# Recurrent mixer: merge levels 1 to 6 as 64x64 diagonal blocks, and half of the convolution's channels for 22 of 31 taps on POOL

## The chip, the cores and the metric

The kernel runs on one core of one Trainium2 chip. The metric is the device time of one execution in microseconds, median of three runs. The engines are TensorE (PE, its weight loads PEld), VectorE (DVE), ScalarE (ACT), GpSimd (POOL) and SyncE (SP, which issues loads).

## The reference, cut to what matters

Two blocks of two layers each work on 256 tokens of 1024 numbers. The change touches one mixer of the second block only, `mixer_ab` of layer 0: a recurrence (RWKV-7) over 8 heads of 64, and beside it a causal depthwise convolution of 31 taps over 512 channels.

```python
def step(state, inp):                       # rwkv7_scan, one token
    r_t, w_t, k_t, v_t, kk_t, a_t = inp
    s_kk = jnp.einsum('bhvk,bhk->bhv', state, kk_t)
    state = (state * w_t[:, :, None, :]
             - s_kk[..., None] * (kk_t * a_t)[:, :, None, :]
             + v_t[..., None] * k_t[:, :, None, :])
    y_t = jnp.einsum('bhvk,bhk->bhv', state, r_t)
    return state, y_t
...
glu = c_val * jax.nn.sigmoid(c_gate)
conv = lax.conv_general_dilated(
    glu, conv_w[:, None, :], window_strides=(1,), padding=[(CONV_WIDTH - 1, 0)],
    dimension_numbers=('NWC', 'WIO', 'NWC'), feature_group_count=D_CONV) + conv_b
y_b = jax.nn.silu(layer_norm(conv, conv_ln_g, conv_ln_b, CONV_LN_EPS))
return jnp.concatenate([y_a, y_b], axis=-1) @ w_out
```

Everything is float32.

## The kernel before, in words

The kernel works in one pass over all layers; nearly all of its time is dense products of weights that stream in (three products each, high and low parts, L2093 to L2095). The recurrent mixer has one stretch of another kind, and it is the one that the change touches.

**The recurrence as block algebra.** The 256 tokens are two blocks of 128. For each block and head the recurrence becomes the inverse of a unit lower triangular 128x128 matrix N. 16 of them (2 blocks, 8 heads) stand in four groups of four: `N_t[g]`, g from 0 to 3, each 128 partitions x 4 x 128. `D_t[g]` and `DT_t[g]` hold the inverse of the diagonal blocks so far and its transpose, `Z_t[g]` a masked product. Level 0 inverts blocks of 2 tokens; level m, from 1 to 6, merges blocks of 2^m into blocks of 2^(m+1). Level 6 joins two halves of 64 to 128, so that levels 1 to 5 never leave the two diagonal 64x64 blocks.

**A step i.** 24 steps, i from 0 to 23, run in an order written out by hand: `merge_group(i)` is 2*(i//12) + i%2 and `merge_level(i)` is i%12//2 + 1, so two groups alternate through their levels, then the other two. Step i consists of: `z_products(i)`, four 128x128 products N by D into a bank (PE); `masked(...)`, which takes the bank through the level's mask into `Z_t` (DVE, L1786); `merge_products(i)`, four products for D and four for DT (PE, `four_products`, L2619; only DT at level 6); `copied(...)`, which takes each into `D_t` and `DT_t` (ACT, L1018). `z_products(i + 2)` waits for D of step i.

**PE's order.** For p from 0 to 10: `merge_products` of 2p and 2p+1, `z_products` of 2p+2 and 2p+3, then other work of the mixer: for p below 6 two `fill`s (Gram matrices, L2609 and L2614, which DVE takes in `take_gram`, L1822 and L1827), after that `first_block_out` (L2644, L2657, L2670, L2650). Then steps 22 and 23 merge, the second block is solved, and the convolution is turned (`convT`, L2719) after a wait for `conv_done`.

**DVE's order.** Per step: `masked`, then some taps of the convolution, then on odd steps two `take_gram`. `tap(j)` is four instructions, one for each group of 128 channels (`ct`), each a `scalar_tensor_tensor` of 128x256 from `gluT` (in `y`) into `conv_o` (in the arena), L1799 (L1796 for j = 0); `taps_at(i)` says how many taps a step has, 31 in all from step 2 to step 21. At step 21 stand `first_state`, the end of the convolution (`conv_done`) and the bonus sum (L1875, `bonus_done`).

**POOL's order.** POOL makes `r_t` (L572, L579, `rk_made`), then waits for `bonus_done` and makes the output's other terms (four products, L572 and L585, `post_made`), then a power for the heads and one for each half of the convolution's norm (`rstd`, L469), for which DVE waits at L1913. The helper `product` waits for its own semaphore after each instruction.

In the masks (`constants()`, c_masks) level m has 128 columns of its own.

Of the kernel before, what the change touches and what calls it, by code (L numbers as in the profile page):

```python
# [83 lines left out]
def program(nc, a, out):  # L84
# [143 lines left out]
    conv_o = part(7168, 4, T)  # L228
    rho = part(8192, TB, RW)
# [35 lines left out]
    merge_m = [pair_m] + [gflat[:, (2 + m) * P:(3 + m) * P] for m in range(6)]  # L265
# [17 lines left out]
    def merge_level(i):  # L283
        return i % 12 // 2 + 1

# [173 lines left out]
    def _(pool):  # L459
# [119 lines left out]
        pool.tensor_tensor(r_t, r_t, both(r_k), ALU.mult).then_inc(SEM["rk_made"], 1)  # L579
        pool.wait_ge(SEM["bonus_done"], c.next("bonus_done"))  # L580
# [40 lines left out]
    def _(act):  # L621
# [394 lines left out]
        def copied(dst, i, at, got, to):  # L1016
            act.wait_ge(SEM[got], c.next(got))
            act.activation(dst[merge_group(i)], bank[at + i % 2][:, :].rearrange("p (a t) -> p a t", a=4), ACT.Copy)\  # L1018
               .then_inc(SEM[to], 1)
# [18 lines left out]
        for i in range(24):  # L1038
            if merge_level(i) < 6:
                copied(D_t, i, 4, "d_mm", "d_ready")  # L1040
            copied(DT_t, i, 6, "dt_mm", "dt_ready")
# [149 lines left out]
    def _(dve):  # L1191
# [600 lines left out]
        def tap(j):  # L1792
            for ct in range(4):
                dve.wait_ge(SEM["dve"], c.so_far("dve") - 3)
# [54 lines left out]
        def taps_at(i):  # L1849
            if i < 2 or i > 21:  # L1850
                return 0
            return 2 if i > 3 and (i % 2 or i in (18, 20)) else 1

        j = 0
        for i in range(24):
            masked(Z_t[merge_group(i)], z_bank[i % 2], merge_m[merge_level(i)], "z_mm", "zp_ready")
# [10 lines left out]
            for _ in range(taps_at(i)):  # L1867
                tap(j)
                j += 1
            if i == 21:  # L1870
# [217 lines left out]
    def _(pe):  # L2088
# [528 lines left out]
        def four_products(bk, left, right, to):  # L2617
            for i in range(4):
                ins = pe.matmul(bank[bk][:, i * P:(i + 1) * P], left[:, i, :], right[:, i, :], start=True, stop=True)  # L2619
            ins.then_inc(SEM[to], 1)  # L2620

        def z_products(i):
            g = merge_group(i)
            if merge_level(i) > 1:
                pe.wait_ge(SEM["d_ready"], c.next("d_ready"))
            four_products(z_bank[i % 2], N_t[g], D_t[g], "z_mm")
# [6 lines left out]
        def merge_products(i):  # L2633
# [4 lines left out]
            if merge_level(i) < 6:  # L2638
                four_products(4 + i % 2, DT_t[g], Z_t[g], "d_mm")
            four_products(6 + i % 2, Z_t[g], DT_t[g], "dt_mm")  # L2640
# [315 lines left out]
```

## Time and profile before

| | us |
|---|---|
| median of 3 runs (lowest, highest) | 2383.51 (2381.48, 2385.42) |
| the profiled execution | 2382.13 |
| its span | 2380.3 |
| busy in the span: PE, DVE, ACT, POOL | 2335.3, 1788.5, 1197.8, 120.6 |

The span runs from the first to the last instruction of the core; the execution's own time has 1.8 us more around it. A line of the timeline names start, length, engine, line of the kernel, operation, destination and sources, and how many instructions are joined in it; in brackets stands the idle time before it and who ended it. Times are microseconds from the span's start. An instruction's length on DVE and ACT runs beside the start of the next one, so that joined lines are shorter than the sum of their parts.

### The profile page before, as it was taken

To read this page: it belongs to the slowest core of one execution; us is meant where nothing else is said; L and a number is where in the kernel's file an instruction comes from. 1 tells how busy PE (TensorE), PEld (TensorE's weight loads), DVE (VectorE), ACT (ScalarE), POOL (GpSimd) and SP (SyncE) were. 2 spreads that over 40 slices of the span, in tenths; PEclk is the share of its full clock that TensorE was granted. 3 is DMA by queue.
4 is the path that set the end of the run, shared out by engine and by line. 5 is a ranking of instruction groups with operands and counts; after the bars stand their busy time and mean duration, and the time that the engine had idled before them with its cause. 6 is when DMAs were issued, how large, how long until landed. Compare 5 with 4: busy or idle time off the path is not lost.

```text
span 2380.3 us, 27847 instructions
## 1 busy us (share of the span) xinstructions
PE 2335.3 (98%) x11426; PEld 1932.5 (81%) x11426; DVE 1788.5 (75%) x1849; ACT 1197.8 (50%) x1413; POOL 120.6 (5%) x145
## 2 busy tenths in 40 slices
PE   9999999999999999999999999999999999999998
PEld 8888877888878888788887887798888888777887
DVE  7875867787787756677787876797877777656875
ACT  5553455365455443644554554534455455555453
POOL 0001000000000010000001002102000000110000
PEclk9999999999999999999999999999999999999999
DMA  9566534565555655365564666304466466343563
GB/s 307 176 229 205 181 106 169 185 218 190 194 188 191 231 197 179 124 225 172 198 225 147 202 210 221 93 1 142 159 213 230 159 212 213 124 159 129 173 200 117
DMA packets 281439, 428.10 MB, mean 180 GB/s; under 512 B 11795, under 2 KB 193683, under 8 KB 281184
## 3 DMA queue, kind: packets, MB, share of 16 engines
q1 hardware_dynamic: 273136, 399.51, 49.6%
q0 software_dynamic: 7632, 26.29, 3.5%
q8 instruction: 90, 1.47, 0.3%
q10 hardware_dynamic: 544, 0.52, 0.1%
q14 instruction: 37, 0.30, 0.0%
HBM read 423.41 MB, written 1.05 MB: 178 GB/s over the span
## 4 chain that ended last, share of the span: by engine, by line
PE 76%; DVE 13%; ACT 5%; DMA 3%; issue 2%; POOL 1%; SPq 0%; POOLq 0%; DVEq 0%; ACTq 0%
PE bank L2093 18%; PE bank L2095 18%; PE bank L2094 18%; DVE wl L1199 6%; PE bank L2185 4%; PE bank L2189 4%; PE bank L2188 4%; ACT wh L629 2%; PE bank L2619 2%; DMA wf<-in_ffn_w_up 1%; PE bank L2140 1%; DMA wf<-in_ffn_w 1%; POOL rstd L469 1%; DVE arena L1799 1%; PE bank L2162 1%
## 5 line engine op out<-in xcount | busy, mean ns | idle before, releaser
L2093 PE MATMUL bank<-wh,xTh 128*128 128x512 f32 x1824 | 723.2, 396 | 9.8 <-DVE xTl L1252 4.0
L1199 DVE TENSOR_TENSOR wl<-wf,wh 128x2048 fp32r<-128x2048 f32 x267 | 605.8, 2286 | 162.6 <-ACT wh L629 162.2
L2095 PE MATMUL bank<-wh,xTl 128*128 128x512 f32 x1824 | 710.0, 389 | 0.0
L2094 PE MATMUL bank<-wl,xTh 128*128 128x512 f32 x1824 | 709.0, 389 | 0.0
L629 ACT ACTIVATE wh<-wf 128x2048 fp32r<-128x2048 f32 x267 | 506.7, 1915 | 175.7 <-PE bank L2095 67.3
L2093 PEld LDWEIGHTS bank<-wh,xTh 128*128 128x128 f32 x1824 | 342.9, 188 | 81.4 <-DVE xTl L1252 5.3
L2095 PEld LDWEIGHTS bank<-wh,xTl 128*128 128x128 f32 x1824 | 342.6, 188 | 72.6
L2094 PEld LDWEIGHTS bank<-wl,xTh 128*128 128x128 f32 x1824 | 343.3, 188 | 67.4 <-issue 0.7
L2093 PE MATMUL bank<-wh,hTh 128*128 128x512 f32 x704 | 277.3, 394 | 0.2
L2095 PE MATMUL bank<-wh,hTl 128*128 128x512 f32 x704 | 275.1, 391 | 0.0
L2094 PE MATMUL bank<-wl,hTh 128*128 128x512 f32 x704 | 274.8, 390 | 0.0
L1199 DVE TENSOR_TENSOR wl<-arena,wh 128x2048 fp32r<-128x2048 f32 x86 | 196.0, 2287 | 46.1 <-ACT wh L629 46.1
L629 ACT ACTIVATE wh<-arena 128x2048 fp32r<-128x2048 f32 x78 | 149.2, 1915 | 70.5 <-PE bank L2095 32.2
L2095 PEld LDWEIGHTS bank<-wh,hTl 128*128 128x128 f32 x704 | 132.5, 188 | 27.9
L2093 PEld LDWEIGHTS bank<-wh,hTh 128*128 128x128 f32 x704 | 132.6, 188 | 27.3 <-DVE wl L1199 0.6
L2094 PEld LDWEIGHTS bank<-wl,hTh 128*128 128x128 f32 x704 | 132.6, 188 | 26.8
L1205 DVE TENSOR_TENSOR wl<-wf,wh 128x2048 fp32r<-128x2048 f32 x64 | 143.5, 2283 | 0.0
L640 ACT ACTIVATE wh<-wf 128x2048 fp32r<-128x2048 f32 x64 | 122.4, 1913 | 34.3 <-PE bank L2095 34.3
L469 POOL TENSOR_TENSOR rstd<-ve,mhalf 128x1 f32<-128x1 f32 x42 | 36.8, 877 | 1625.4 <-DVE ve L1278 809.3
L2185 PE MATMUL bank<-wh,wh 128*128 128x512 f32 x256 | 100.4, 392 | 1.0 <-ACT y L644 0.6
L2189 PE MATMUL bank<-wh,wl 128*128 128x512 f32 x256 | 99.7, 389 | 0.0
L2188 PE MATMUL bank<-wl,wh 128*128 128x512 f32 x256 | 99.6, 389 | 0.0
(368 smaller groups left out, 2589.9 us busy)
## 6 DMA issues: line engine op xcount, KB each, us to landing
wf<-in_ffn_w SPq DMA_DIRECT2D x136, 512.0 KB, 6.0
wf<-in_w_in SPq DMA_DIRECT2D x52, 1024.0 KB, 5.6
wf<-in_ffn_w_gate SPq DMA_DIRECT2D x68, 512.0 KB, 5.9
wf<-in_ffn_w_up SPq DMA_DIRECT2D x68, 512.0 KB, 6.9
wf<-in_ffn_w SPq DMA_DIRECT2D x28, 1024.0 KB, 7.1
wf<-in_ffn_w_down SPq DMA_DIRECT2D x28, 1024.0 KB, 7.7
arena<-in_ffn_w SPq DMA_DIRECT2D x38, 512.0 KB, 7.8
arena<-in_ffn_w SPq DMA_DIRECT2D x16, 1024.0 KB, 5.9
```

The costliest lines, as they stand in the source:

```text
L469: pool.tensor_tensor(dst, src, mhalf[:, 0:n], ALU.pow).then_inc(SEM[to], 1)
L629: act.activation(wh[s], wf[s], ACT.Copy).then_inc(SEM[f"hi{s}"], 1)
L640: act.activation(wh[s], src, ACT.Copy).then_inc(SEM[f"hi{s}"], 1)
L1199: dve.tensor_tensor(wl[s], wf[s], wh[s].bitcast(f32), ALU.subtract).then_inc(SEM[f"lo{s}"], 1)
L1205: dve.tensor_tensor(wl[s], src, wh[s].bitcast(f32), ALU.subtract).then_inc(SEM[f"lo{s}"], 1)
L2093: pe.matmul(o, lh, rh, start=start, stop=False)
L2094: pe.matmul(o, lh, rl, start=False, stop=False)
L2095: return pe.matmul(o, ll, rh, start=False, stop=stop)
L2185: ins = pe.matmul(o, lh, wh[s][:, r], start=start and q == 0, stop=False, skip_group_check=not start)
L2188: pe.matmul(o, lh, wl[s][:, r], start=False, stop=False, skip_group_check=not start)
L2189: ins = pe.matmul(o, ll, wh[s][:, r], start=False, stop=q == 3, skip_group_check=not start)
L2619: ins = pe.matmul(bank[bk][:, i * P:(i + 1) * P], left[:, i, :], right[:, i, :], start=True, stop=True)
```

## The change: blocks on PE, half of the channels on POOL

- `four_products` becomes `block_products`: eight products of 64x64 for a group instead of four of 128x128, on the two diagonal quarters of the array, into 256 columns of a bank instead of 512. `D_t` and `Z_t` are kept packed in 64 columns; DT keeps its place. Level 6 is four products of 64x64 for Z and four for DT, in one quarter each.
- DVE's mask and ACT's copies take 128x256 instead of 128x512 (level 6: 64 partitions). At level 5 DT is taken in two instructions of 64 partitions.
- POOL computes channels 256 to 511 (`ct` 2 and 3) for taps 0 to 21, as a multiplication and an addition of 128x2x256 for each tap, 44 instructions, after `rk_made` and ahead of its wait for `bonus_done`. The products go through `tap_o`, in the second half of `beta`.
- DVE computes channels 0 to 255 for all 31 taps in steps 2 to 20, and channels 256 to 511 for taps 22 to 30 in steps 18 to 21, after a wait at step 18 for POOL's `conv_done`. PE waits for both engines' `conv_done`.
- Tap instructions of DVE wait for the one before the last instead of for the fourth last.

```diff
+    tap_o = part(6656, 2, T)
+    POOL_TAPS = 22
...
-    merge_m = [pair_m] + [gflat[:, (2 + m) * P:(3 + m) * P] for m in range(6)]
+    merge_m = [pair_m] + [gflat[:, (2 + m) * P:(2 + m) * P + HD] for m in range(5)]
...
+
+        def weight(j):
+            return convw[:, 2:4, j:j + 1].broadcast_to([P, 2, T])
+
+        pool.wait_ge(SEM["gluT_ready"], c.next("gluT_ready", TB))
+        pool.wait_ge(SEM["cw_ready"], c.next("cw_ready"))
+        pool.wait_ge(SEM["gram_ready"], c.next("gram_ready", 4))
+        product(conv_o[:, 2:4, :], gluT[:, 2:4, 0:T], weight(0))
+        product(conv_o[:, 2:4, :], conv_o[:, 2:4, :], weight(CONV), ALU.add)
+        for j in range(1, POOL_TAPS):
+            product(tap_o, gluT[:, 2:4, j:j + T], weight(j))
+            product(conv_o[:, 2:4, :], conv_o[:, 2:4, :], tap_o, ALU.add)
+        pool.sem_inc(SEM["conv_done"], 1)
         pool.wait_ge(SEM["bonus_done"], c.next("bonus_done"))
...
+        def d_copied(i):
+            act.wait_ge(SEM["d_mm"], c.next("d_mm"))
+            act.activation(D_t[merge_group(i)][:, :, 0:HD], blocks(4 + i % 2), ACT.Copy).then_inc(SEM["d_ready"], 1)
+
+        def dt_copied(i):
+            act.wait_ge(SEM["dt_mm"], c.next("dt_mm"))
+            dst, src = DT_t[merge_group(i)], blocks(6 + i % 2)
+            if merge_level(i) < 5:
+                ins = act.activation(dst[:, :, HD:P], src, ACT.Copy)
+            elif merge_level(i) == 5:
+                act.activation(dst[0:HD, :, 0:HD], src[0:HD, :, :], ACT.Copy)
+                ins = act.activation(dst[HD:P, :, HD:P], src[HD:P, :, :], ACT.Copy)
+            else:
+                ins = act.activation(dst[0:HD, :, HD:P], src[0:HD, :, :], ACT.Copy)
+            ins.then_inc(SEM["dt_ready"], 1)
...
+        def tap(j, groups):
+            for ct in groups:
+                dve.wait_ge(SEM["dve"], c.so_far("dve") - 1)
                 if j == 0:
                     ins = dve.tensor_scalar(conv_o[:, ct, :], gluT[:, ct, 0:T], convw[:, ct, 0:1], convw[:, ct, CONV:CONV + 1],
                                             ALU.mult, ALU.add)
...
         def taps_at(i):
-            if i < 2 or i > 21:
-                return 0
-            return 2 if i > 3 and (i % 2 or i in (18, 20)) else 1
+            return 0 if i < 2 or i > 20 else 1 if i in (2, 4, 6, 8, 10, 12, 14) else 2
...
+        def merged(i):
+            dve.wait_ge(SEM["z_mm"], c.next("z_mm"))
+            dst, src = Z_t[merge_group(i)][:, :, 0:HD], blocks(z_bank[i % 2])
+            if merge_level(i) < 6:
+                ins = dve.tensor_tensor(dst, src, merge_m[merge_level(i)].rearrange("p (a n) -> p a n", a=1).broadcast_to([P, 4, HD]),
+                                        ALU.mult)
+            else:
+                ins = dve.tensor_copy(dst[HD:P, :, :], src[HD:P, :, :])
+            ins.then_inc(SEM["zp_ready"], 1)
...
+        LATE_TAPS = {18: range(22, 24), 19: range(24, 26), 20: range(26, 28), 21: range(28, CONV), 22: (), 23: ()}
         for i in range(24):
-            masked(Z_t[merge_group(i)], z_bank[i % 2], merge_m[merge_level(i)], "z_mm", "zp_ready")
+            merged(i)
...
             for _ in range(taps_at(i)):
-                tap(j)
+                tap(j, range(2))
                 j += 1
+            if i == 18:
+                dve.wait_ge(SEM["conv_done"], c.next("conv_done"))
+            if i > 17:
+                for k in LATE_TAPS[i]:
+                    tap(k, range(2, 4))
...
+        halves = [slice(o * HD, (o + 1) * HD) for o in range(2)]
+
+        def block_products(bk, left, left_at, right, right_at, to):
+            for q in range(4):
+                for o, f in enumerate(halves):
+                    ins = pe.matmul(bank[bk][f, q * HD:(q + 1) * HD], left[f, q, halves[left_at[o]]], right[f, q, halves[right_at[o]]],
+                                    start=True, stop=True)
             ins.then_inc(SEM[to], 1)
...
         def z_products(i):
-            g = merge_group(i)
-            if merge_level(i) > 1:
+            g, level = merge_group(i), merge_level(i)
+            if level > 1:
                 pe.wait_ge(SEM["d_ready"], c.next("d_ready"))
-            four_products(z_bank[i % 2], N_t[g], D_t[g], "z_mm")
+            if level < 6:
+                block_products(z_bank[i % 2], N_t[g], (0, 1), D_t[g], (0, 1) if level == 1 else (0, 0), "z_mm")
+            else:
+                for q in range(4):
+                    ins = pe.matmul(bank[z_bank[i % 2]][HD:P, q * HD:(q + 1) * HD], N_t[g][0:HD, q, HD:P], D_t[g][0:HD, q, 0:HD],
+                                    start=True, stop=True)
+                ins.then_inc(SEM["z_mm"], 1)
...
             if merge_level(i) < 6:
-                four_products(4 + i % 2, DT_t[g], Z_t[g], "d_mm")
-            four_products(6 + i % 2, Z_t[g], DT_t[g], "dt_mm")
+                turned_at = (0, 1) if merge_level(i) == 1 else (1, 1)
+                block_products(4 + i % 2, DT_t[g], turned_at, Z_t[g], (0, 0), "d_mm")
+                block_products(6 + i % 2, Z_t[g], (0, 0), DT_t[g], turned_at, "dt_mm")
+            else:
+                for q in range(4):
+                    ins = pe.matmul(bank[6 + i % 2][0:HD, q * HD:(q + 1) * HD], Z_t[g][HD:P, q, 0:HD], DT_t[g][HD:P, q, HD:P],
+                                    start=True, stop=True)
+                ins.then_inc(SEM["dt_mm"], 1)
...
-        pe.wait_ge(SEM["conv_done"], c.next("conv_done"))
+        pe.wait_ge(SEM["conv_done"], c.next("conv_done", 2))
...
-        masks.append((merged | (r[:, None] == r[None, :])).astype(f))
+        mask = (merged | (r[:, None] == r[None, :])).astype(f)
+        if 0 < m < 6:
+            mask[HD:, 0:HD] = mask[HD:, HD:]
+            mask[:, HD:] = 0
+        masks.append(mask)
```

## Rows read from the trace of the kernel before

**Rows 1.** Windows of the merges' stretch: length, PE, PEld, DVE, ACT, POOL busy, PEclk, DMA share, GB/s.
```profile
1541.00:1556.00 15.00, 14.97 (x122) 14.10 (x123) 9.59 (x20) 4.78 (x8) 4.57 (x2) 1.00 0.14 34
...
1570.00:1583.00 13.00, 12.85 (x97) 11.79 (x97) 13.00 (x30) 3.58 (x6) 0.00 (x0) 1.00 0.00 0
```

**Rows 2.** Timeline, DVE at step 2, PE and DVE over one pair, DVE at step 18.
```profile
1545.87 0.69 DVE L1786 TENSOR_TENSOR wf<-bank,gains 128x512 f32<-128x512 f32 x1 [5.01 <-PE bank L2619]
...
1570.37 5.62 PE L2619 MATMUL bank<-wf 128*128 128x128 f32 x48
1570.74 3.25 DVE L1799 SCALAR_TENSOR_TENSOR arena<-y,arena 128x256 f32<-128x256 f32 x8
...
1575.93 1.99 PE L2609 MATMUL bank<-rows_T 64*128 64x256 f32 x8
...
1603.28 0.69 DVE L1786 TENSOR_TENSOR wf<-bank,gains 128x512 f32<-128x512 f32 x1 [1.11 <-PE bank L2619]
```

**Rows 3.** Groups by line and form, 1540 to 1625 us: count, busy us, mean ns.
```profile
L1799 DVE SCALAR_TENSOR_TENSOR arena<-y,arena 128x256 f32<-128x256 f32 x120 | 49.0, 475 | 0.1
...
L1786 DVE TENSOR_TENSOR wf<-bank,gains 128x512 f32<-128x512 f32 x22 | 14.9, 683 | 7.8 <-PE bank L2619 7.8
...
L1822 DVE TENSOR_TENSOR arena<-bank,gains 128x512 f32<-128x512 f32 x8 | 5.1, 678 | 0.0
```

**Rows 4.** Timeline, DVE and POOL at the stretch's end.
```profile
1620.21 1.22 DVE L1875 TENSOR_REDUCE gains<-arena 128x16 f32<-128x1024 f32 x1 [0.15 <-DVE arena L1799]
...
1621.51 2.16 POOL L572 TENSOR_TENSOR arena<-arena,gains 128x512 f32<-128x512 f32 x2 [75.86 <-DVE gains L1875]
...
1633.55 0.56 POOL L469 TENSOR_TENSOR rstd<-ve,mhalf 128x1 f32<-128x1 f32 x1 [0.43 <-DVE ve L1897]
...
1634.16 1.41 DVE L1913 SCALAR_TENSOR_TENSOR arena<-arena,rstd 128x512 f32<-128x512 f32 x2
```

**Rows 5.** Timeline, small products on PE: rows of 64 in turn, columns of 64 in turn.
```profile
1525.27 2.06 PE L2583 MATMUL bank<-rows_T 64*128 64x128 f32 x32 [0.34 <-ACT rows_T L1013]
...
1604.06 1.15 PE L2670 MATMUL bank<-arena 128*64 128x64 f32 x32
```

**Rows 6.** Groups by form, whole span: DVE and ACT on 128x256 from a bank.
```profile
L1706 DVE TENSOR_TENSOR y<-bank,arena 128x256 f32<-128x256 f32 x2 | 0.8, 420 | 2.7 <-PE bank L2095 2.7
...
L958 ACT ACTIVATE arena<-bank 128x256 f32<-128x256 f32 x2 | 0.7, 382 | 6.6 <-DVE y L1710 6.6
```

**Rows 7.** Timeline, POOL's two products before its long wait.
```profile
1540.86 2.36 POOL L572 TENSOR_TENSOR arena<-arena 128x1024 f32<-128x1024 f32 x1
...
1543.30 2.35 POOL L579 TENSOR_TENSOR arena<-arena,row 128x1024 f32<-128x1024 f32 x1
```

**Rows 8.** Timeline: DVE beside POOL's cast, and beside its products.
```profile
2059.29 1.89 POOL L610 CAST wh<-arena 128x2048 fp32r<-128x2048 f32 x1
...
2057.77 0.69 DVE L1947 TENSOR_TENSOR y<-y,arena 128x512 f32<-128x512 f32 x1 [0.96 <-POOL arena L469]
2059.37 2.35 DVE L1947 TENSOR_TENSOR y<-y,arena 128x512 f32<-128x512 f32 x1 [0.91 <-POOL arena L469]
...
1621.46 1.29 DVE L1786 TENSOR_TENSOR wf<-bank,gains 128x512 f32<-128x512 f32 x2
```

**Rows 9.** Timeline: POOL's power beside DVE's statistics (246) and beside L1281 (184).
```profile
246.21 1.27 DVE L1274 BATCH_NORM_STATS2 stats<-arena 128x6 f32<-128x512 f32 x2
...
246.38 0.56 POOL L469 TENSOR_TENSOR rstd<-ve,mhalf 128x1 f32<-128x1 f32 x1 [32.24 <-DVE ve L1278]
...
184.15 1.28 DVE L1281 SCALAR_TENSOR_TENSOR y<-y,mv,gains 128x1024 f32<-128x1024 f32 x1
...
184.31 1.53 POOL L469 TENSOR_TENSOR rstd<-ve,mhalf 128x1 f32<-128x1 f32 x1 [159.85 <-DVE ve L1278]
```

**Rows 10.** Windows: the clock before and after a thin stretch of PE (columns as in rows 1).
```profile
1530.00:1536.00 6.00, 3.29 (x26) 2.87 (x27) 5.98 (x8) 1.08 (x2) 0.00 (x0) 1.00 0.00 0
1536.00:1539.00 3.00, 3.00 (x17) 3.00 (x16) 2.04 (x4) 0.50 (x1) 0.00 (x0) 0.50 0.02 5
```

More of the change, by code:

```diff
@@ L284, in merge_level, with blocks @@
         return i % 12 // 2 + 1
+    def blocks(b):
+        return bank[b][:, 0:4 * HD].rearrange("p (a t) -> p a t", a=4)
     def heads(t):
@@ L1014, in take_rows @@
                            bank[bk][:, :].rearrange("p (q w t) -> p q w t", q=2, w=2), ACT.Copy).then_inc(SEM["rows_ready"], 1)
[L1016 to L1019, printed above, removed]
+        def d_copied(i):
[12 more added lines that the diff above has]
+            ins.then_inc(SEM["dt_ready"], 1)
         def taken(dst, b, bk, got, to):
@@ L1039, in _ @@
             if merge_level(i) < 6:
-                copied(D_t, i, 4, "d_mm", "d_ready")
-            copied(DT_t, i, 6, "dt_mm", "dt_ready")
+                d_copied(i)
+            dt_copied(i)
             if i == 13:
@@ L1790, in with_identity @@
             dve.tensor_tensor(N_t[g], N_t[g], four(ident[:, :]), ALU.add).then_inc(SEM["n_ready"], 1)
-        def tap(j):
-            for ct in range(4):
-                dve.wait_ge(SEM["dve"], c.so_far("dve") - 3)
+        def tap(j, groups):
+            for ct in groups:
+                dve.wait_ge(SEM["dve"], c.so_far("dve") - 1)
                 if j == 0:
@@ L2615, in fill @@
             ins.then_inc(SEM["gram_mm"], 1)
-        def four_products(bk, left, right, to):
-            for i in range(4):
-                ins = pe.matmul(bank[bk][:, i * P:(i + 1) * P], left[:, i, :], right[:, i, :], start=True, stop=True)
+        halves = [slice(o * HD, (o + 1) * HD) for o in range(2)]
[4 more added lines that the diff above has]
+                                    start=True, stop=True)
             ins.then_inc(SEM[to], 1)
         def z_products(i):
-            g = merge_group(i)
-            if merge_level(i) > 1:
+            g, level = merge_group(i), merge_level(i)
+            if level > 1:
                 pe.wait_ge(SEM["d_ready"], c.next("d_ready"))
-            four_products(z_bank[i % 2], N_t[g], D_t[g], "z_mm")
+            if level < 6:
[5 more added lines that the diff above has]
+                ins.then_inc(SEM["z_mm"], 1)
         def first_turned(g):
```

## The prediction, made before the change was run

> **What bounds the kernel now.** I read the windows of the stretch first, then the timeline of one pair of steps, then the groups by form for the prices, then the end of the stretch. In the first 15 us PE is busy for 14.97 and DVE for 9.59; from 1570 on DVE is busy for 13.00 of 13.00 and PE for 12.85 [rows 1]. So two engines are full at once. Step 2's mask starts at 1545.87 and step 18's at 1603.28, eight pairs in 57.4 us, 7.2 each [rows 2]. PE's pair is 24 products in 5.62 and fills of about 1.9 (7.5); DVE's is two masks at 0.61 start to start (two take 1.29 [rows 8]), twelve tap instructions at 0.40 (eight take 3.25 [rows 2]) and two Gram masks in 1.3 (0.68 each [rows 3]): 7.3. A tap alone lasts 0.475 [rows 3], but its neighbour starts earlier.
>
> At the end, the bonus sum ends on DVE at 1621.43, POOL starts at once and its chain of four products, a power and two rstd runs without a real gap to 1634.11; L1913 starts at 1634.16 [rows 4]. So the end of the stretch lies 12.7 us behind the bonus sum, and nothing in that chain is changed. What the change is worth is how far the bonus sum moves from 1621.4.
>
> From step 18's mask to the bonus sum's end are 18.15 us: four masks 2.4, 32 tap instructions 12.8, the sum 1.2; the 1.7 left is `first_state`.
>
> **The blocks on PE.** A group of products becomes eight of 64x64, 16 records. Products with 64 weight columns and 64 moving columns, in alternate columns of the array, take 1.15 us for 32 records, 0.036 each; products on 64 rows in turn, but 128 columns wide, 2.06 for 32, 0.064 each [rows 5]. The first is nearest in width and in moving columns: 16 x 0.036 = 0.58 for a group, against 5.62/6 = 0.94 before; the other end is 16 x 0.064 = 1.03. Six groups and fills: 3.5 + 1.9 = 5.4 for a pair instead of 7.5 (at the other end 8.1). Level 6, in one quarter, is 8 records and costs no more than 0.58.
>
> **Copies and masks.** DVE's 128x256 from a bank lasts 0.42 and ACT's 0.38 [rows 6]; start to start I take 0.35 for the mask instead of 0.61. ACT has idle time in every pair (4.78 busy of 15 [rows 1]), so its copies, and the second one at level 5, cost nothing; without that cover they would cost 0.4 each at four steps. Earlier start: Z of steps 0 and 1 is some 1.2 us shorter at most, and moves the first merge by up to that; POOL does not start earlier for it, so I count it as 0 and keep 1 us for the range. The tighter wait between taps costs nothing: the one before the last has ended (0.475) when the next is due (0.80).
>
> **Taps on DVE.** Six instead of twelve instructions a pair: 0.7 + 2.4 + 1.3 = 4.4 us, were DVE alone. From step 18's wait on: 26 taps 10.4, three masks 1.05, `first_state` 1.7, the sum 1.2: 14.4 us.
>
> **POOL.** It starts at 1545.7, behind its product that ends at 1545.65 [rows 7]. A multiplication of 128x512 with a repeated factor lasts 1.04 (two take 2.16 [rows 4]); 128x1024 with two full sources lasts 2.36, half of it 1.18; 0.08 lies between two of them [rows 7]. 44 instructions at 1.11 + 0.08: 52.4 us, to 1598.1 (all at 1.04: 1595.0; all at 1.18: 1601.1). It has no queue behind it but the bonus terms. Nobody but DVE at step 18 and PE at `convT` waits for it.
>
> **Do taps and POOL exclude one another?** This decides. A DVE instruction with two SBUF sources, issued 0.08 behind a POOL cast of 1.89, took 2.35 instead of 0.69: it ended 0.54 behind the cast [rows 8]. POOL's power takes 0.56 beside a DVE instruction that reads one tensor, and 1.53 beside L1281, which reads two: it ended at 185.84, 0.41 behind L1281 [rows 9]. DVE's masks, with one source in a bank, lost nothing beside POOL (1.29 for two, from 1621.46 [rows 8]). Taps read two SBUF tensors, and POOL's products read SBUF throughout. So I take it that one waits for the other, with 0.15 of its start hidden: a tap ends 0.33 behind the product that held it up, a product 0.96 behind the tap. No row has a tap beside a product. The Trainium skill (SBUF — State Buffer, Who interferes with whom) says that a VectorE instruction with two SBUF inputs and a GpSimd one that reads SBUF shut each other out for the whole instruction; by that, case 3 below would lose its chance to cases 1 and 2.
>
> **Case 1, they take turns (0.42, the forecast).** A met tap and a product together take 0.33 + 0.96 = 1.29, so POOL loses 0.10 for each; DVE gets a tap only every 1.29. On DVE two taps cost 0.55 (half a product) + 0.33 + 1.29 = 2.2 and four cost 4.75; a pair of steps 0.7 + 1.3 + 6.95 = 8.9. POOL, with some 38 met taps, ends at 1598.1 + 3.8 = 1602. By then DVE has done (1602 - 1545.7)/8.9 = 6.3 pairs and stands at the end of step 15. Left are 38 taps 15.2, six masks 2.1, `first_state` and the sum 2.9: 20.2; the pair of 16 and 17 is PE's (5.4 against 3.9), 1.5 more. The sum ends at 1623.7, 2.3 later than before. The profiled execution's 2382.1 becomes 2384.4; the median of the runs lies 1.4 above that execution, and I say 2385. What each engine gained the lock gives back. Its own range: 44 x 0.07 of POOL's price either way is 3, the early start 1, the blocks at 1.03 are case 4: 2379 to 2391.
>
> **Case 2, DVE's queued taps go through together (0.20), slower.** The place is POOL's queue: it loses 0.33 + 0.40(n-1) + 0.96 - 1.19 for a group of n, 0.50 for two and 1.30 for four. Seven groups of two and ten of four before step 18's wait: 16.5. POOL ends at 1614.6, DVE stands at step 18 from about 1590, and the sum ends 14.4 later, at 1629.0: +7.6, 2390 to 2391. It decides from the point where POOL loses more than about 8.9 us. For it: DVE's tap starts before its neighbour has ended; against: nothing.
>
> **Case 3, taps and products hardly meet (0.18), faster.** POOL ends at 1598.1, the sum at 1612.5: 8.9 earlier, 2373 to 2375. For it: only that no row has these two forms side by side.
>
> **Case 4, TensorE (0.15), slower.** The blocks at 1.03 make a pair 8.1, and the last three pairs, which have 6.7 in case 1, become 4 us longer: +6. Or the clock: behind a stretch with PE busy for 3.29 of 6.00 us the granted clock fell to 0.50, the lower of its two levels, for 3 us [rows 10]. In case 1 PE is busy for 5.4 of 8.9; at half clock a pair is 10.8, and three such pairs add 5.7. Both give 2388 to 2391. In rows 5 the 64-row products went to different banks in turn, and the column ones used all rows. The Trainium skill (TensorEngine Tiling (Array Packing), Restrictions and Gotchas) says that different row tiles cannot access one bank at the same time; here both quarters write one bank, in different partitions, and by that rule the +6 would be the sum.
>
> The last 0.05 is for what I don't see.
>
> **The numbers.** About 0.2%, 4.8 us, is what a measurement of this kernel can tell from no change: 2378.7 to 2388.3. Faster: case 3 and a tenth of case 1, 0.23. Slower: most of cases 2 and 4 (0.24) and a quarter of case 1, 0.37 with the rest. The same: 0.40. The range reaches from the middle of case 3 to the far end of cases 2 and 4: 2374 to 2392.
>
> **What would show it.** Tap instructions of well over 0.475 us while POOL works, up to 1.3; POOL's products at about 1.1 in case 1, many at 1.5 to 2.3 in case 2, none in case 3. POOL's last product at 1602, 1615 or 1598. DVE's wait at step 18: none, 20 us or more, about 10. Groups of products at 0.58 (16 records) and a clock of 1.00. The bonus sum at 1623.7, with 12.7 us from there to L1913. I am wrong if tap instructions keep their length beside POOL, or if the chain behind the bonus sum is not what ends the stretch.

## The result, and the profile after

The changed kernel takes 2386.59 us (median of 20 runs, 2383.81 to 2388.77) against 2382.32 for the kernel before (20 runs, 2378.84 to 2385.42): a ratio of 1.0019, 95% interval 1.0012 to 1.0025. It is slower by 4.3 us, just under the 0.2% that I had called measurable (the interval excludes "no change"), and 1.6 above the 2385.0 that I had forecast. The 2385 held 1.4 for the distance of the median of before, then of three runs, from its profiled execution, and with twenty runs that distance is 0.2. The change itself was forecast at +2.3 and measured +4.3. Below, one execution of the first experiment, 3867.14 us at a mean granted clock of 0.555, is left out as a slow one.

The execution that the profile shows has a span of 2387.0 us, 6.7 above that of before; it is the slowest of the twenty, 2.2 above their median. Of the 6.7, 2.9 are there when the bonus sum ends (1624.31 instead of 1621.43 [rows 4]), 2.3 more when the first half of the convolution's norm starts (L1956, which is L1913 of before: 1639.34 instead of 1634.16), and 1.5 come later, in code that is the same; the runs of one kernel differ by more than that. The 2.9 needs care, because the two executions enter the stretch at different times: POOL's first product of `r_t`, which the change doesn't touch, starts at 1540.86 in before [rows 7] and at 1539.09 in after. From that product on, the sum's end is 80.6 away in before and 85.2 in after, 4.7 more.

Timeline of the kernel after, POOL and DVE in the steps 5 to 8. L577 is POOL's product, L1828 a tap of DVE, L1851 a Gram mask, L1885 the mask of a merge.

```profile
1558.39 1.33 POOL L577 TENSOR_TENSOR arena<-arena 128x512 f32<-128x512 f32 x1
1559.80 1.10 POOL L577 TENSOR_TENSOR arena<-y,arena 128x512 f32<-128x512 f32 x1
...
1559.92 1.26 DVE L1828 SCALAR_TENSOR_TENSOR arena<-y,arena 128x256 f32<-128x256 f32 x1
1561.10 1.28 DVE L1851 TENSOR_TENSOR arena<-bank,gains 128x512 f32<-128x512 f32 x2
1562.30 0.41 DVE L1885 TENSOR_TENSOR wf<-bank,gains 128x256 f32<-128x256 f32 x1
1562.63 2.48 DVE L1828 SCALAR_TENSOR_TENSOR arena<-y,arena 128x256 f32<-128x256 f32 x2
1565.03 0.41 DVE L1885 TENSOR_TENSOR wf<-bank,gains 128x256 f32<-128x256 f32 x1
1565.37 4.92 DVE L1828 SCALAR_TENSOR_TENSOR arena<-y,arena 128x256 f32<-128x256 f32 x4
...
1571.41 0.41 DVE L1885 TENSOR_TENSOR wf<-bank,gains 128x256 f32<-128x256 f32 x1
```

The tap issued at 1559.92, 0.12 behind the start of a product, ends at 1561.18, 0.28 behind the product's end (1560.90). Four taps in a row take 4.92, where eight took 3.25 before [rows 2]. Masks that read one source from a bank keep their length (0.41, and two Gram masks 1.28). From 1562.30 to 1571.41 is one pair of steps: 9.1 us. The same groups while POOL works:

```profile
L1828 DVE SCALAR_TENSOR_TENSOR arena<-y,arena 128x256 f32<-128x256 f32 x36 | 43.3, 1255 | 0.1
L577 POOL TENSOR_TENSOR arena<-arena 128x512 f32<-128x512 f32 x22 | 28.7, 1305 | 1.7
L577 POOL TENSOR_TENSOR arena<-y,arena 128x512 f32<-128x512 f32 x22 | 24.9, 1131 | 1.6
```

These are groups by line and form from 1543 to 1601: a tap lasts 1.255 on average instead of 0.475 [rows 3]. POOL's products take 53.6 for 44, which gives 1.22 each.

Timeline, POOL's last product and DVE behind it:

```profile
1598.28 0.41 DVE L1885 TENSOR_TENSOR wf<-bank,gains 128x256 f32<-128x256 f32 x1
...
1599.48 1.33 POOL L577 TENSOR_TENSOR arena<-arena 128x512 f32<-128x512 f32 x1
...
1601.01 0.41 DVE L1885 TENSOR_TENSOR wf<-bank,gains 128x256 f32<-128x256 f32 x1
1601.35 1.66 DVE L1828 SCALAR_TENSOR_TENSOR arena<-y,arena 128x256 f32<-128x256 f32 x4
...
1608.01 0.42 DVE L1885 TENSOR_TENSOR wf<-bank,gains 128x256 f32<-128x256 f32 x1 [0.95 <-PE bank L2665]
1608.36 3.25 DVE L1828 SCALAR_TENSOR_TENSOR arena<-y,arena 128x256 f32<-128x256 f32 x8
```

1598.28 is step 14's mask, 1601.01 step 15's, 1608.01 step 18's. POOL is done at 1600.81, and the very next four taps take 1.66 again. At step 18 DVE waits 0.95 for PE and not for POOL, which had finished 7 us earlier. Windows of the stretch (length, then busy time of PE, PEld, DVE, ACT, POOL, the granted clock, DMA share, GB/s):

```profile
1541.00:1556.00 15.00, 8.70 (x149) 7.68 (x146) 14.46 (x15) 1.88 (x5) 14.22 (x12) 0.86 0.03 9
1556.00:1570.00 14.00, 11.16 (x202) 9.61 (x201) 14.00 (x16) 3.07 (x8) 13.22 (x11) 0.78 0.01 1
1570.00:1583.00 13.00, 9.21 (x104) 8.16 (x104) 12.94 (x16) 2.28 (x6) 12.14 (x12) 0.72 0.00 1
1583.00:1598.00 15.00, 12.12 (x154) 10.04 (x152) 14.90 (x18) 2.29 (x6) 14.14 (x12) 0.56 0.01 2
1598.00:1614.00 16.00, 14.19 (x352) 13.52 (x352) 14.91 (x35) 5.80 (x14) 2.65 (x3) 1.00 0.01 3
1614.00:1629.00 15.00, 13.82 (x175) 13.29 (x172) 13.84 (x31) 4.26 (x10) 4.44 (x3) 0.93 0.12 32
```

Against [rows 1] PE has idle time now, and DVE is full from 1556 to 1598 with 50 instructions in 42 us, where it had 30 in 13. DVE and POOL look both busy all the time: part of each one's busy time is waiting for the other inside an instruction, which these columns can't tell from work. PE's busy share is lower, and its granted clock falls to 0.56.

### The profile page after: what moved, and what is told of

Its sections match the earlier page's. It is cut to its first block, busy times and chain, and to the rows that moved or that the text cites. A ratio compares the mean times of both kernels' runs of the same rounds, so it can differ in the third digit from the quotient of the medians.

```text
span 2387.0 us, 28814 instructions
## 1 busy us (share of the span) xinstructions
PE 2321.9 (97%) x11906; PEld 1916.9 (80%) x11906; DVE 1796.3 (75%) x1805; ACT 1190.2 (50%) x1417; POOL 174.2 (7%) x189
## 3 DMA queue, kind: packets, MB, share of 16 engines
HBM read 423.41 MB, written 1.05 MB: 178 GB/s over the span
## 4 chain that ended last, share of the span: by engine, by line
PE 75%; DVE 15%; ACT 4%; DMA 2%; issue 2%; POOL 1%; SPq 0%; DVEq 0%; POOLq 0%; ACTq 0%
PE bank L2136 19%; PE bank L2138 18%; PE bank L2137 18%; DVE wl L1228 6%; PE bank L2228 4%; PE bank L2232 4%; PE bank L2231 4%; DVE arena L1828 2%; ACT wh L647 2%; DMA wf<-in_ffn_w_up 1%; PE bank L2183 1%; DMA wf<-in_ffn_w 1%; POOL rstd L474 1%; PE bank L2205 1%; PE bank L2455 1%
```

## The experiments

Ten kernels ran. The sum's end is the end of the bonus sum in the profiled execution, and the tail is the time from there to the start of the norm's first half (12.7 in the kernel before). Each ratio is to runs of before that were taken with it, whose medians are 2382.32, 2382.94 (1 to 4), 2381.77 (5 to 8) and 2382.28 (9 and 10). One profile stands behind each row, and the executions enter the stretch up to 5 us apart (POOL's first product at 1537.20 in the seventh, 1542.72 in the ninth), so that the column of the sum's end compares only roughly.

| kernel | median us | ratio to before | sum's end | tail |
|---|---|---|---|---|
| after | 2386.59 | 1.0019 [1.0012, 1.0025] | 1624.31 | 15.0 |
| 1 blocks alone | 2374.20 | 0.9971 [0.9959, 0.9984] | 1613.23 | 12.6 |
| 2 split alone | 2395.75 | 1.0058 [1.0041, 1.0075] | 1633.54 | 13.6 |
| 3 no products on POOL | 2359.35 | one run | 1595.78 | 15.4 |
| 4 POOL writes only | 2370.32 | one run | 1610.13 | 11.8 |
| 5 sums in a bank | 2377.24 | 0.9987 [0.9976, 0.9998] | 1613.72 | 11.8 |
| 6 clock kept, after | 2388.37 | 1.0028 [1.0019, 1.0037] | 1627.79 | 13.7 |
| 7 clock kept, blocks | 2374.58 | 0.9969 [0.9957, 0.9981] | 1610.28 | 11.8 |
| 8 sums in a bank, 16 taps | 2365.07 | 0.9927 [0.9913, 0.9940] | 1603.33 | 12.7 |
| 9 clock kept at the end | 2386.33 | 1.0019 [1.0010, 1.0027] | 1627.96 | 13.4 |
| 10 sums in a bank, 14 taps | 2366.60 | 0.9932 [0.9916, 0.9947] | 1606.27 | 13.5 |

### 1 and 2: each half of the change by itself

The blocks alone, from the kernel after (POOL's products gone, DVE's taps in the old order and with their old wait):

```diff
-            return 0 if i < 2 or i > 20 else 1 if i in (2, 4, 6, 8, 10, 12, 14) else 2
+            if i < 2 or i > 21:
+                return 0
+            return 2 if i > 3 and (i % 2 or i in (18, 20)) else 1
...
-                tap(j, range(2))
+                tap(j, range(4))
```

> The blocks stay, all four channel groups of the convolution go back to DVE with the schedule of before, POOL computes nothing of it. Exclusion theory (the taps and POOL's products shut each other out, and that alone eats the gain): taps at 0.475 us, 0.40 start to start, a pair of steps 0.7 + 4.8 + 1.3 = 6.8 us on DVE; from step 2's mask at about 1541.5 the bonus sum is reached after 68 us, at 1610, 11 us earlier than before: about 2371. Rival (the blocks themselves bring nothing, because the granted clock falls when PE has less to do): windows at 0.50, a pair at 7 us or more, the sum between 1617 and 1622, 2378 to 2383.

The split alone, from the kernel before (128x128 products stay; POOL's 44 products, `LATE_TAPS` and the wait at step 18 as in the change):

```diff
-                tap(j)
+                tap(j, range(2))
+            if i == 18:
+                dve.wait_ge(SEM["conv_done"], c.next("conv_done"))
+            if i > 17:
+                for k in LATE_TAPS[i]:
+                    tap(k, range(2, 4))
```

> The 128x128 products stay, only the convolution is split between DVE and POOL as in the change. Exclusion theory: taps beside POOL take up to 1.3 us, a pair costs DVE 1.2 + 1.3 + 7.0 = 9.5 us until POOL ends near 1602, then PE's 7.5 a pair: the sum near 1629, 7 to 9 us later than before, about 2390; PE is busy for 7.5 of 9.5 and the clock stays at 1.00 most of the time. Rival (the split is harmless and the loss is the blocks' falling clock): taps at 0.475, the sum near 1617, 2378 or less.

Measured against the same runs of before (2382.94): the blocks give 8.7 back, the split costs 12.8. Together that makes +4.1, and the whole change measured +4.3. So what looks like a change with hardly an effect is a gain and a larger loss. That they add up so closely is in part chance: the intervals are 3.8 to 9.8 us for the gain and 9.8 to 17.9 for the loss. Both kernels came slower than I had expected (2371 and 2390). In the split alone DVE waits for PE's larger products at steps 18 and 20, behind POOL's end (3.48 and 2.69 us), so that its loss isn't the taps' alone.

The timeline of the blocks alone, one pair of steps:

```profile
1557.05 0.42 DVE L1878 TENSOR_TENSOR wf<-bank,gains 128x256 f32<-128x256 f32 x1
...
1559.29 3.26 DVE L1819 SCALAR_TENSOR_TENSOR arena<-y,arena 128x256 f32<-128x256 f32 x8
...
1563.65 0.43 DVE L1878 TENSOR_TENSOR wf<-bank,gains 128x256 f32<-128x256 f32 x1
```

The pair takes 6.6 instead of 7.2, on DVE: twelve taps at their full speed and two cheaper masks. And of the split alone:

```profile
1556.38 0.68 DVE L1801 TENSOR_TENSOR wf<-bank,gains 128x512 f32<-128x512 f32 x1
...
1556.98 2.21 DVE L1814 SCALAR_TENSOR_TENSOR arena<-y,arena 128x256 f32<-128x256 f32 x2
...
1559.71 4.66 DVE L1814 SCALAR_TENSOR_TENSOR arena<-y,arena 128x256 f32<-128x256 f32 x4
...
1565.50 0.68 DVE L1801 TENSOR_TENSOR wf<-bank,gains 128x512 f32<-128x512 f32 x1
```

Here the pair takes 9.1 with half of the taps. The long taps come with the split and not with the blocks.

### 3 and 4: is it what POOL reads?

In both, POOL's 44 products are gone, so that taps 0 to 21 of channels 256 to 511 are left out of the convolution. The third kernel has one memset in their place, the fourth has 88, each of the same 128x512 that a product writes:

```diff
-        product(conv_o[:, 2:4, :], gluT[:, 2:4, 0:T], weight(0))
-        product(conv_o[:, 2:4, :], conv_o[:, 2:4, :], weight(CONV), ALU.add)
-        for j in range(1, POOL_TAPS):
-            product(tap_o, gluT[:, 2:4, j:j + T], weight(j))
-            product(conv_o[:, 2:4, :], conv_o[:, 2:4, :], tap_o, ALU.add)
+        for b in range(88):
+            pool.memset(conv_o[:, 2:4, :], 0.0).then_inc(SEM["made"], 1)
+            pool.wait_ge(SEM["made"], c.next("made"))
```

> The change without POOL's 44 products: one memset of channels 256 to 511 stands in their place, so taps 0 to 21 of those channels are left out. Exclusion theory: every tap at 0.475, a pair is PE's 5.4 us, the bonus sum near 1597, some 24 us before the kernel before: about 2358. Rival (taps are slowed by something else than POOL, the semaphore wait for the one before the last or the clock): taps keep lengths of 1.2 to 1.3 us and the sum stays beyond 1610.

> The change with 88 memsets of POOL in place of its 44 products, so that POOL is as long at work but reads nothing of SBUF; taps 0 to 21 of channels 256 to 511 are left out. If what excludes is the reading of a second SBUF source: taps at 0.475 beside the memsets, DVE at step 18 before 1592 and waiting for POOL. If any access of POOL shuts a tap out: taps wait for a memset's end, about 0.5 to 0.9 us each, and step 18 comes near 1600.

Groups by form from 1547 to 1583, first of the kernel without products, then of the one that writes only:

```profile
L1826 DVE SCALAR_TENSOR_TENSOR arena<-y,arena 128x256 f32<-128x256 f32 x52 | 21.9, 482 | 0.1
```

```profile
L1826 DVE SCALAR_TENSOR_TENSOR arena<-y,arena 128x256 f32<-128x256 f32 x50 | 21.1, 481 | 0.1
...
L593 POOL MEMSET arena<- 128x512 f32 x63 | 33.0, 524 | 3.6
```

Without products a tap is 0.482, and beside 63 memsets, with POOL busy for 33 of 36 us, it is 0.481. From step 3's mask to step 18's DVE takes 36.32 in both (1543.18 to 1579.50, and 1545.67 to 1581.99): POOL's writing costs DVE nothing. The two kernels differ by 11.0 us, with one run of each. The main term is DVE's wait for POOL at step 18, 11.77 (this is how the wait looks when POOL is late); against it stand 3.6 in the tail, 15.4 in the third kernel and 11.8 in the fourth, for which see the clock below:

```profile
1581.99 0.42 DVE L1883 TENSOR_TENSOR wf<-bank,gains 128x256 f32<-128x256 f32 x1 [0.95 <-PE bank L2663]
...
1595.76 1.67 DVE L1826 SCALAR_TENSOR_TENSOR arena<-y,arena 128x256 f32<-128x256 f32 x4 [11.77 <-POOLq L595]
```

So neither POOL's being busy nor its writes hold up a tap. What its products have beside these is that they read from SBUF.

### 5: one of the tap's sources in a bank

If the exclusion needs two SBUF sources on DVE's side, a tap whose running sum lies in PSUM should meet POOL unharmed. D and DT of a step share a bank, which frees bank 6 for the sums of channels 0 to 255; POOL still has 22 taps, and nothing is left out:

```diff
+        def acc(ct):
+            return bank[6][:, ct * T:(ct + 1) * T] if ct < 2 else conv_o[:, ct, :]
...
-                    ins = dve.scalar_tensor_tensor(conv_o[:, ct, :], gluT[:, ct, j:j + T], convw[:, ct, j:j + 1],
-                                                   conv_o[:, ct, :], ALU.mult, ALU.add)
+                    ins = dve.scalar_tensor_tensor(conv_o[:, ct, :] if j == CONV - 1 else acc(ct), gluT[:, ct, j:j + T],
+                                                   convw[:, ct, j:j + 1], acc(ct), ALU.mult, ALU.add)
...
-                block_products(4 + i % 2, DT_t[g], turned_at, Z_t[g], (0, 0), "d_mm")
-                block_products(6 + i % 2, Z_t[g], (0, 0), DT_t[g], turned_at, "dt_mm")
+                block_products(4 + i % 2, DT_t[g], turned_at, Z_t[g], (0, 0), None)
+                block_products(4 + i % 2, Z_t[g], (0, 0), DT_t[g], turned_at, "dt_mm", 256)
```

> The change, but DVE's running sums of channels 0 to 255 stand in a PSUM bank instead of SBUF, so that a tap has one SBUF source; D and DT of a step share a bank to make room, POOL keeps its 22 taps. Exclusion by the second SBUF source: taps keep 0.42 to 0.48 us beside POOL, POOL's products take 1.04 to 1.10 each, POOL ends near 1596, DVE waits for it at step 18, the bonus sum ends near 1610, about 2371. Rival (any DVE instruction on SBUF data is held up by POOL's products): taps at 1.2 to 1.3 as in the change, the sum near 1624, 2386.

Groups by form from 1547 to 1583, and the end of DVE's wait:

```profile
L1831 DVE SCALAR_TENSOR_TENSOR bank<-y,arena,bank 128x256 f32<-128x256 f32 x49 | 20.6, 482 | 0.1
...
L577 POOL TENSOR_TENSOR arena<-arena 128x512 f32<-128x512 f32 x15 | 19.7, 1312 | 1.2
L577 POOL TENSOR_TENSOR arena<-y,arena 128x512 f32<-128x512 f32 x15 | 15.6, 1041 | 1.2
```

```profile
1599.38 1.67 DVE L1831 SCALAR_TENSOR_TENSOR arena<-y,arena 128x256 f32<-128x256 f32 x4 [14.80 <-POOLq L597]
```

With the same products beside them the taps last 0.482 instead of 1.255. POOL's multiplications go back to 1.04, its additions to 1.27 (the mean holds one of 1.90 beside L1756, which has two SBUF sources). The edit moves the tap's result to the bank too, so by itself it doesn't say which of the two moves helps. The masks do: L1885 and L1851 read one source from a bank and one from SBUF and write to SBUF, and beside the same products they keep their length (0.41, and 1.28 for two). So a result in SBUF doesn't hold them up, and what the tap has lost is its second SBUF source.

DVE is now at step 18 by 1582.6 and waits 14.8 us for POOL. This kernel's median is 2377.24 over ten runs that spread from 2373.79, the profiled one, to 2386.42, and its interval only just excludes "no change": the wait has taken most of the gain. Why its runs spread so much isn't shown.

### 8 and 10: fewer taps for POOL

The wait of 14.8 us says that POOL has too much. POOL's tap is 2.49 us in the fifth kernel (1544.50 to 1599.29 for 22), and each that goes to DVE costs that engine two instructions at 0.40. The eighth kernel takes 16 taps on POOL, moves DVE's own taps to steps 2 to 17, its late ones to steps 16 to 21 and its wait to step 16; the tenth takes 14.

```diff
-    POOL_TAPS = 22
+    POOL_TAPS = 16
...
-            return 0 if i < 2 or i > 20 else 1 if i in (2, 4, 6, 8, 10, 12, 14) else 2
+            return 0 if i < 2 or i > 17 else 1 if i == 2 else 2
...
-            if i == 18:
+            if i == 16:
```

> As the one with the sums in a bank, but POOL takes 16 taps instead of 22, DVE's own taps end at step 17 and it takes the late ones in steps 16 to 21. Exclusion by the second source: POOL ends near 1582 and DVE hardly waits; a pair is 5.2 to 5.5 us, the bonus sum ends near 1602, 2362 to 2366, the fastest so far. Rival: as in the change, taps of 1.2 us until POOL ends, the sum beyond 1612.

> As the one with the sums in a bank and 16 taps on POOL, with 14. POOL ends 5 us earlier, near 1580, DVE's wait of 2.9 us at step 16 goes away, and DVE has four late tap instructions more (1.6 us). If DVE bounds from step 16 on: 1 to 1.5 us faster, 2364; if PE does: no difference, 2365.

The timeline with 16 taps, at the wait and at the end:

```profile
1585.14 1.68 DVE L1831 SCALAR_TENSOR_TENSOR arena<-y,arena 128x256 f32<-128x256 f32 x4 [2.89 <-POOLq L597]
...
1602.11 1.22 DVE L1921 TENSOR_REDUCE gains<-arena 128x16 f32<-128x1024 f32 x1 [0.15 <-DVE arena L1831]
...
1616.03 1.41 DVE L1959 SCALAR_TENSOR_TENSOR arena<-arena,rstd 128x512 f32<-128x512 f32 x2
```

The wait is down to 2.9, the sum ends 18 us earlier than before, and the kernel takes 2365.07: 17 us less than before and 21.5 less than the change. With 14 taps DVE no longer waits for POOL, but the kernel takes 2366.60. With four runs of each the two can't be told apart. Both beat the kernel before and the kernel after.

The profile of the tenth kernel shows where its 2.9 us went. By the price above, 1.6 are the four late tap instructions that it has more. The larger part is PE's: from 1570 to 1578 the granted clock is 0.50, where the eighth kernel has 1.00, a merge pair of 96 records takes PE 4.95 instead of 3.25, the Gram products before it 3.78 instead of 1.99, and DVE waits at step 14, as it doesn't with 16 taps:

```profile
1579.27 0.42 DVE L1888 TENSOR_TENSOR wf<-bank,gains 128x256 f32<-128x256 f32 x1 [2.71 <-PE bank L2668]
```

Step 12 to step 14 takes 7.8 instead of 5.0.

### 6, 7 and 9: what does TensorE's clock cost?

The granted clock of after is well below 1.00 in four windows. Idle products (`busy`) behind each pair of steps keep PE working. The sixth kernel puts eight behind each pair of after, the seventh four behind each pair of the blocks alone, the ninth eight behind the last two pairs of after only:

```diff
+            if p > 8:
+                busy(8, 4, ident[:, :])
```

> The change with eight idle products of 128 columns on PE ahead of the fills of each pair, which fill some 1.9 us of the 3.5 that PE waits in a pair. If the lower clock costs what the tail shows (12.7 us behind the bonus sum became 15.0, and the rest is hidden behind DVE): the clock near 1.00, the sum still at 1623 to 1625, the tail back at 12.7, 2 to 2.5 us faster than the change, 2384. If the clock costs nothing: 2386.6. If it also held up the stretch itself: 2380 or less.

> Blocks alone, all taps on DVE, with four idle products of 128 columns on PE per pair, which PE's waits have room for (5.4 + 0.9 us against DVE's 6.8). If the clock at 0.56 between 1570 and 1583 held up the steps: 1 to 2 us faster than blocks alone, 2373. If it was hidden behind DVE: the same 2374.4 within 0.5 us.

> The change with eight idle products on PE only ahead of the last two pairs' other work (p = 9 and 10), where PE waits for DVE. If the end's 15.0 us behind the bonus sum are 12.7 plus a clock of 0.50: the clock at 1.00 behind the sum, 12.7 to 13.2 there, the sum where it was (1624), 2384 to 2385. If the 2.3 us come from elsewhere (DVE's or POOL's order at the end): 2386.6, with the clock at 1.00.

A window of the sixth, to be compared with the same of after:

```profile
1583.00:1598.00 15.00, 12.90 (x176) 11.90 (x176) 14.91 (x17) 2.10 (x6) 14.06 (x13) 0.77 0.01 2
```

The clock rises from 0.56 to 0.77 where it was lowest, and DVE is as full as before: 14.91 of 15. PE waits for DVE there, so that its slower products are covered: from step 2's mask to step 15's it is 59.50 in after and 59.55 in the sixth. So the clock cost nothing in these steps of after. The time doesn't get better, 2388.37 against 2386.59, and the sum isn't where I expected it either, because the idle products cost something themselves. Behind POOL's end PE is the slower engine, and DVE waits for it 1.47 at step 16 and 2.74 at step 18, where after has none and 0.95:

```profile
1611.49 0.42 DVE L1885 TENSOR_TENSOR wf<-bank,gains 128x256 f32<-128x256 f32 x1 [2.74 <-PE bank L2665]
```

These 3.3 hide the 1.3 that the tail gives back (13.7 for 15.0). With the blocks alone the clock goes from 0.56 to 0.74 in 1570 to 1583 and the time stays (2374.58 against 2374.20), but not because the clock was free: DVE's wait for PE at step 14 falls from 1.13 to 0.53, and the idle products take it back by step 18. Where DVE has little to spare, as in the tenth kernel above, the low clock costs 2.7 us inside the stretch, in the one execution that shows it.

Behind the bonus sum it's another matter. In after PE idles for 1.05 us, and the clock is at its lower level from about 1627.5 to 1637. From there the timeline is:

```profile
1624.82 1.14 PE L2697 MATMUL bank<-wf 64*64 64x64 f32 x16 [1.05 <-DVE wf L1888]
...
1633.57 1.91 PE L2778 MATMUL bank<-ident,arena 128*128 128x128 f32 x8
...
1635.52 0.70 DVE L1937 BATCH_NORM_STATS2 stats<-bank 128x6 f32<-128x512 f32 x1 [6.51 <-PE bank L2778]
...
1636.82 0.56 POOL L474 TENSOR_TENSOR rstd<-ve,mhalf 128x1 f32<-128x1 f32 x1 [1.36 <-DVE ve L1940]
...
1639.34 1.42 DVE L1956 SCALAR_TENSOR_TENSOR arena<-arena,rstd 128x512 f32<-128x512 f32 x2
```

The turned convolution (L2778) is PE's, eight products in 1.91 where the ninth kernel, at a clock of 1.00, has them in 1.04. The norm's statistics wait 6.51 for it, and POOL's rstd waits for the statistics. So two chains run behind the sum, POOL's of [rows 4] and one of PE that begins with the last merge (L2697), and the longer one ends the stretch. POOL's by itself is 11.8 long and not 12.7, as the fourth, fifth and seventh kernels show, where its two rstd stand back to back (here the fifth):

```profile
1624.86 1.05 POOL L474 TENSOR_TENSOR rstd<-ve,mhalf 128x1 f32<-128x1 f32 x2
```

In the kernel before, the second rstd waits 0.43 for DVE's statistics [rows 4], and these for PE's turned convolution: its 12.7 was already PE's chain, whose last merge starts there at 1623.07, 1.6 behind the sum. PE's takes 14.5 from L2697 to L1956 in after (1624.82 to 1639.34). In the ninth kernel, at full clock, it takes 10.5:

```profile
1630.85 1.14 PE L2697 MATMUL bank<-wf 64*64 64x64 f32 x16
...
1636.44 1.04 PE L2780 MATMUL bank<-ident,arena 128*128 128x128 f32 x8
...
1641.34 1.42 DVE L1956 SCALAR_TENSOR_TENSOR arena<-arena,rstd 128x512 f32<-128x512 f32 x2
```

The half clock costs PE's chain 4.0 us. At full clock it would end 11.0 behind the sum in after (0.5 + 10.5), before POOL's 11.8, so that 3.2 of the 4.0 show, 2.3 of them over the 12.7 of before. The third kernel repeats it: PE idle for 1.05 ahead of the last merge, a clock of 0.50 from 1602 to 1607, and a tail of 15.4; the fourth, fifth and seventh have 1.00 there and 11.8. The ninth kernel was to give the cost back, and its median, 2386.33, isn't better by more than the runs differ. Its profile says why at most half could come: the idle products in front put L2697 to 2.9 behind the sum's end instead of 0.5, so that the tail is 2.9 + 10.5 = 13.4. (The whole stretch stood 3.6 later in that execution, POOL's first product at 1547.47; that start differs by so much from one profiled execution to the next, which is why distances are compared here.) The tenth kernel, with no idle products, has L2701, its last merge, 3.0 behind the sum for another reason, PE being late at the end, and the same 10.5 and 13.5. With the blocks alone four idle products a pair did it (the seventh kernel's 11.8 for the first's 12.6); for the whole change neither filling gave the tail back without a cost ahead of it, and no better one was tried.

## Why the prediction was right

**The bound and the measure.** The forecast held in its sign, its range and its main mechanism. That the sum's end lies only 0.6 beside the forecast (+2.9 for +2.3) is luck: the profiled execution entered the stretch 1.8 earlier than that of before, and from POOL's first product on the sum came 4.7 later. One sign of being wrong that I had named did come true: the chain behind the bonus sum isn't what ends the stretch (below, the tail).

**The blocks** took 3.02 to 3.25 for 96 records at full clock, 0.50 to 0.54 for a group, where I had 0.58. At a clock of 0.50 96 records take 5.38. The far end, 0.064 a record, didn't come: both quarters write one bank, in different partitions, at 0.031 a record. At level 6, where one quarter works alone, 16 records take 1.14 (L2697), 0.071 each, so that two quarters in turn are no slower for sharing a bank. The Trainium skill (TensorEngine Tiling (Array Packing), Restrictions and Gotchas) has it that different row tiles cannot access one bank at the same time. The price that I had tied to it didn't come; whether both quarters ever wrote at the same moment these rows don't show, so that the rule itself isn't tested. By themselves the blocks are worth 8.7 us.

**Masks and copies.** Start to start 0.34 (1601.01 to 1601.35), against 0.35; ACT's copies were covered.

**The lock and the turns.** The step that decided held. A tap and the product that it meets took 1.295 together (2.59 us for two products and two taps), where I had 0.33 + 0.96 = 1.29; two taps 2.14 to 2.48 against 2.2, four 4.67 to 5.13 against 4.75, a pair of steps 8.8 to 9.1 against 8.9, but for the first. Taps never went through together (case 2): one tap goes between two products. Kernels 3 to 5 show that it takes a product that reads SBUF on one side and a second SBUF source on the other. The Trainium skill (SBUF — State Buffer, Who interferes with whom) says just this, that a GpSimd instruction which only writes is free of it too, and the traces agree (0.481 beside memsets); that the two engines take turns stands on these rows alone.

**POOL.** Two sizes were off and cancelled. With taps that don't meet it, an addition is 1.27 (1.18 forecast), so that 22 taps are 54.3 and not 52.4; a met product loses 0.06 and not 0.10 (1.10 for 1.04, 1.33 for 1.27). From its first product to its last POOL took 57.0, against 56.3. It started 1.8 earlier than forecast (1543.84 for 1545.7), but that isn't the change's doing: its `r_t` products ahead of it are 1.8 earlier as well, and in the ninth kernel, whose code is the same up to there, it started at 1547.47. That POOL doesn't start earlier for the shorter products, as the prediction had it, holds.

**DVE at POOL's end.** This is the step that was worked wrongly. I counted 6.3 pairs from step 2's mask and put DVE at the end of step 15, but 6.3 pairs end inside step 14. Measured, DVE was at the end of step 14 (1601.0), and from POOL's end to the sum's end were 23.5 us where I had 21.7, nearly one step more. Together with the 0.7 of POOL's longer work that is the difference between 4.7 and 2.3. That DVE wasn't further behind still it owes to its start: step 2's mask is at 1541.51, not at 1545.87. 1.8 of these 4.4 us are the execution's, 2.6 the shorter products of steps 0 and 1, for which I had at most 1.2. They paid for something else that I had left out, the first pair of 11.9 us: two `tensor_scalar` taps of 3.23 beside POOL's products for `r_t`, and L1756, with two SBUF sources, 1.79 instead of 1.21.

```profile
1541.51 0.42 DVE L1885 TENSOR_TENSOR wf<-bank,gains 128x256 f32<-128x256 f32 x1 [2.42 <-PE bank L2665]
1541.53 2.35 POOL L584 TENSOR_TENSOR arena<-arena,row 128x1024 f32<-128x1024 f32 x1
1541.85 3.23 DVE L1825 TENSOR_SCALAR arena<-y,arena 128x256 f32<-128x256 f32 x2
...
1545.34 1.79 DVE L1756 TENSOR_TENSOR arena<-arena 128x1024 f32<-128x1024 f32 x1
```

**The tail.** "With 12.7 us from there to L1913" failed: 15.0. I had read [rows 4] as POOL's chain "without a real gap", but the gap of 0.43 in it is the sign that PE's chain came last already in the kernel before. Nothing in POOL's chain was changed, and PE's beside it was. I had the clock's fall as part of case 4 and put its cost into the last pairs of steps. It fell, to 0.56, cost nothing in the steps up to POOL's end, and cost 3.2 in the tail, where I had no term for PE at all.

**The sum of it.** Counted from POOL's first product, +4.7 and +2.3 make +7.0 at the end of the stretch in these two executions. The medians differ by 4.3; the profiled execution of after is 2.2 above its median, and which part of the stretch is shorter in the others no profile shows. So the mechanism of case 1 was right, step by step, and two terms were short: DVE's place at POOL's end by 1.8, and PE in the tail by 2.3.

## What to carry to other kernels

Before work goes to POOL beside DVE, count the SBUF sources of what DVE does at that time: with two of them each instruction paid here for one of POOL's, and half of the taps cost more than all of them had. Accumulating in PSUM, where a bank could be freed, is what made POOL a second engine: with a share that leaves hardly a wait, that kernel is 9 us faster than the blocks alone, and 17 faster than before. A change of two parts that hardly moves the time should be run part by part: here one gives 8.7 us and the other takes 12.8. And a tail that "isn't changed" should be checked for a second chain beside it: a short idle time in the last link is its sign.

## What the runs showed of the hardware that I had not expected

- A DVE instruction with only one source is held up as well if it is a `tensor_scalar` from SBUF to SBUF: two of them took 3.23 beside a product of POOL (L1825 above), where four took 1.37 in the kernel before, with POOL idle (406 ns for one). With its result going to a bank the pair took 0.99 (0.540 for one) in the fifth kernel, where that product (L584) runs until 1544.54; no run has this form with POOL idle. The Trainium skill (SBUF — State Buffer, Who interferes with whom) names `tensor_scalar` among the operations that can take the shared pair of ports, and the first two numbers agree:

```profile
1543.82 0.99 DVE L1828 TENSOR_SCALAR bank<-y,arena 128x256 f32<-128x256 f32 x2
```

- Turns are strict: wherever taps stood in a row while POOL worked, one tap went between two products (four taps in 4.92, two products and two taps in 2.59), though DVE had the next one waiting.
- POOL's price depends on its sources: 128x512 takes 0.525 to write only, 1.04 with one full source and a repeated factor, 1.27 with two full sources.
- The clock of TensorE fell to 0.50 at 1552, behind four microseconds (1548 to 1552) with PE idle, and its mean was 0.56 from 1583 to 1598, where PE was busy for 12 of 15 us. Idle products brought it up to 0.77 there, but no time. What it costs depends on who waits for PE: nothing where DVE is behind (59.50 and 59.55 to step 15), 2.7 at step 14 of the tenth kernel, 3.2 in the tail.
